# A fourth slot for weight halves, and one slot fewer for gathered rows, in a two-layer decoder step on one core

## The reference

```
h = rmsnorm(x);  proj = h @ w_in                      # 1024 x 2560, and 8 gate columns
mLSTM heads on q, k, v, o;  causal pooling on the last 512 columns
x = x + concat(heads, pooled) @ w_out                 # 1024 x 1024
q = rmsnorm(x) @ wq                                   # 1024 x 2048: 8 heads x 2 halves x 128
s = q . keys;  top 16 of 128 in each half;  top 16 of the 256 sums -> eidx, gate
x = x + sum over 8 heads x 16 experts of gate * gelu(xb . u_tab[eidx]) * v_tab[eidx]
x = x + sigmoid(x @ w_gate) * (p @ w_ple)             # 1024 x 1024, 256 x 1024
```

## Time and profile before

| | |
|---|---|
| median of three runs | 1790.19 us (1785.57 to 1794.6) |
| the profiled execution | 1792.79 us, its span 1790.6 us |
| mean granted TensorE clock | 0.824 |
| PE, DVE, ACT, POOL busy (share of the span) | 76%, 55%, 39%, 28% |
| read from HBM | 679.87 MB |
| mean rate of the DMA engines | 384 GB/s |

### The profile page before, as it was taken

The page is one execution under the profiler, slowest core; times in us unless marked ns, Lnnn a source line. Parts: engine busy times, 40 slices in busy tenths (PEclk is TensorE's granted clock), DMA queues, the critical chain, the costliest instruction groups (busy, mean ns, idle before and its releaser), DMA issues. The chain is left out here.

```text
span 1790.6 us, 19308 instructions
## 1 busy us (share of the span) xinstructions
PE 1364.3 (76%) x6310; PEld 501.9 (28%) x6310; DVE 992.0 (55%) x2540; ACT 692.9 (39%) x1965; POOL 498.0 (28%) x532
## 2 busy tenths in 40 slices
PE   7967689788948879757767897898756677777766
PEld 3523134333413333211113433443311211111113
DVE  1373754756883455875443436668874344555443
ACT  2234435334433453333332645343343333333334
POOL 0031232232222223224332222222333133333330
PEclk9968599889979989986668898899877865676678
DMA  7697699999989999999999799999999989999992
GB/s 309 239 375 306 244 426 428 378 399 426 424 349 377 426 427 417 427 387 392 427 426 422 284 418 421 377 422 416 410 349 427 378 342 427 427 427 427 427 427 116
DMA packets 96737, 687.26 MB, mean 384 GB/s; under 512 B 11104, under 2 KB 12640, under 8 KB 14318
## 3 DMA queue, kind: packets, MB, share of 16 engines
q0 software_dynamic: 76032, 553.68, 74.8%
q1 hardware_dynamic: 20606, 132.36, 18.3%
HBM read 679.87 MB, written 6.59 MB: 383 GB/s over the span
## 5 line engine op out<-in xcount | busy, mean ns | idle before, releaser
L1202 PE MATMUL acc<-rows,weighted 128*64 128x512 f32 x2048 | 699.5, 789 | 268.6 <-ACT weighted L1593 257.2
L2068 DVE SCALAR_TENSOR_TENSOR rows<-rows,shown 128x1024 f32<-128x1024 f32 x528 | 632.7, 1220 | 381.5 <-DMA rows<-in_uv,index_B 249.5
L1399 POOL DMA_INDIRECT rows<-in_uv,index_A x256 | 242.4, 947 | 722.6 <-PE acc L1202 585.7
L889 PE MATMUL bank<-wring,turned 128*128 128x512 f32 (+1 forms) x840 | 385.5, 607 | 8.7 <-DMA wring<-in_w 7.7
L1399 POOL DMA_INDIRECT rows<-in_uv,index_B x256 | 240.4, 939 | 496.6 <-PE acc L1202 474.4
L1202 PEld LDWEIGHTS acc<-rows,weighted 128*64 128x64 f32 x2048 | 134.6, 162 | 731.1 <-ACT weighted L1593 619.7
L889 PEld LDWEIGHTS bank<-wring,turned 128*128 128x128 f32 x840 | 157.7, 196 | 207.6 <-issue 197.3
L1582 ACT ACTIVATE dots_B<-dots_B 128x1 f32<-128x1 f32 x256 | 51.6, 202 | 359.8 <-DVE rows L2068 354.6
L1582 ACT ACTIVATE dots_A<-dots_A 128x1 f32<-128x1 f32 x256 | 51.3, 200 | 267.5 <-DVE rows L2068 253.9
L1593 ACT ACTIVATE weighted<-consts,dots_A 128x64 f32<-128x64 f32 x256 | 89.0, 348 | 8.4
L1593 ACT ACTIVATE weighted<-consts,dots_B 128x64 f32<-128x64 f32 x256 | 89.0, 348 | 8.4
(11 more groups left out here) (312 smaller groups left out, 999.6 us busy)
## 6 DMA issues: line engine op xcount, KB each, us to landing
wring<-in_w SPq DMA_DIRECT2D x107, 1024.0 KB
out_sample<-scratch SPq DMA_DIRECT2D x2, 2128.5 KB, 11.9
scratch<-in_c_s SPq DMA_DIRECT2D x2, 2064.0 KB, 16.0
rows<-in_uv,index_A POOLq DMA_INDIRECT x256
rows<-in_uv,index_B POOLq DMA_INDIRECT x256
keys<-in_keys SPq DMA_DIRECT2D x2, 1024.0 KB
gain<-in_gain SPq DMA_DIRECT2D x3, 640.0 KB
consts<-in_consts SPq DMA_DIRECT2D x1, 1243.0 KB, 11.9
```

The lines of the kernel that those rows point to most:

```text
L889: ins = pe.matmul(ps[:, part], turned["A"][:, 4 * h + c, :], w[:, c, part], start=first, stop=end, skip_group_check=True)
L1202: ins = pe.matmul(acc[c * 64:(c + 1) * 64, :], weighted[:, n % STATS, :], row[:, c * BLOCK:(c + 1) * BLOCK], start=first, stop=end, skip_g ...
L1399: pool.indirect_dma_start(out=rows[:, n % RING, :], out_offset=None, in_=a["uv"], in_offset=bass.IndirectOffsetOnAxis(ap=index[kind][:, pa ...
L2068: dve.scalar_tensor_tensor(u, u, 1.0, shown[:, :, :], ALU.mult, ALU.mult, accum_out=dots[kind][:, part, i:i + 1]).then_inc(u_used, 1)
```

## The change

`RING`, the slots for gathered rows, goes from 8 to 7; `WRING`, the slots for weight halves, from 3 to 4. Both kinds of slot take 8 KB of a partition, so the room is the same. Both numbers also stand in `Clocks`, so the order of stages is made anew by the same rules. The work itself stays the same.

```
-RING = 8
+RING = 7
 STATS = 8
 LANE = 32
 HALF = 2 * P
-WRING = 3
+WRING = 4
```

## The result

The changed kernel takes 1810.55 us (median of 4 runs, 1808.57 to 1812.47) against 1787.88 us for the kernel before beside it: ratio 1.0129, 95% interval 1.0083 to 1.0174, so 23 us slower. The forecast was 1803 with a range of 1785 to 1817. Direction and range hold; the median lies 8 us above the forecast. The profiled execution has a span of 1808.6 us, 18.0 over that of before.

What follows compares the result with a forecast made beforehand. The DMA engines were taken as the bound, with 181 us of lost time to move. Holes 14.8 plus order 3.5 minus start 3.6 minus pass 0 to 1 2.2 made +12.5: forecast 1803 us, range 1785 to 1817.

Steps and rivals of the forecast that it cites:

- A slot less, six holes: DMA holes at 350, 510, 790, 967, 1130, 1290 us: each loses 2.46 us more, sum 14.8, bounds 0 to 17.2.
- What was taken as 0: Pure gather stretches at 0; windows 130 to 220 and 1397 to 1442 us not counted; mixed stretches given no cost.
- The new order: Ranking windows, passes 0 to 2: seven gathers fewer beside the ranking, +3.5 us, bounds -5 to 8.7.
- Start: Before the first index: fourth half already loaded, fifth lands near 29.5, gains 3.6 us, bounds 0 and 4.3.
- Pass 0 to 1: Window 550 to 580 us: fourth half of `gate` resident, PE's wait near 565 gone, gains 2.2 us, low bound 0.
- the two stalls: PE's waits for the fourth half at the start and near 565 us: mending both gives -5.8 us.
- rival (b): 130 to 220 us: new order shortens tile 0's chain by 7 us or more; near 1781, faster; chance 0.14.
- the likeliest case: Whole kernel: gather slots decide, as forecast; own range 1794 to 1816 us; chance 0.55.
- the argument that rests on the pause: SP's pauses in loading halves lie over holes and long stretches, so halves lie ready while gathers are short.
- The signs named beforehand: Changed profile: first gather about 91, no wait near 565, six holes 2 to 3 us larger, 427 GB/s in pure stretches.
- (a): The six holes: room is room, five or more don't grow, only stalls go; 1788 us, no change; chance 0.25.
- (c): Pure gather stretches: seven slots too few, 0.14 us a gather, 36 us in all, 1839 us; chance 0.06.

Runs made afterwards that it cites:

- 7/3: Seven gather slots and three for halves, stage order of the kernel before, against the kernel before: 1821.01 us, ratio 1.0187.
- 7/4: Seven gather slots and four for halves, stage order of the kernel before, against the kernel before: 1817.01 us, ratio 1.0158.
- the limit in one hole: Kernel before (eight and three, its order) with the gather ring seven deep for gathers 104 to 127 only: 1788.03 us, ratio 1.0013.
- the run that limits them: Kernel before with the gather ring seven deep for gathers 32–65, 84–105, 138–189 and 310–349 only: 1802.69 us, ratio 1.0068.
- The second exchange: Six gather slots and five for halves, stage order of the kernel before, against the kernel before: 1863.99 us, ratio 1.0435.
- the run limited in the long stretches: Kernel before with the gather ring seven deep for gathers 208 to 263 and 408 to 527 only: 1786.16 us, ratio 1.0005.

## Why the prediction was right, and where its sum wasn't

*A slot less, six holes, +14.8.* The mechanism was right: the ring is the reserve of the DMA, and a hole that empties it costs one slot more. With the order kept, these holes (gathers 66 to 82, 106 to 136, 190 to 208, 264 to 286, 286 to 318, 350 to 370) lose 1.9 + 4.9 + 2.1 + 0 + 4.6 + 3.0 = 16.5 us more with seven slots (mean of the runs 7/3 and 7/4) than the mean with eight, and the limit in one hole cost 3.0 us of DMA time. Single holes were off: 106 to 136 cost two slots, the one at the pass end showed nothing within its scatter, and its 15.7 us in the profile of before were themselves at the upper end of a scatter from 11.4 to 16.5.

*What was taken as 0.* This is the step of the sum that failed: "Not counted: 130 to 220 [...]; 1397 to 1442" and the silence on the mixed stretches. With the order kept, 0 to 32 and 370 to 410 lose 3.0 and 1.7 us more, and the mixed stretches some 10, shown by the run that limits them and the last gathers of one hole (+12 us, 9.8 us of DMA time in the stretches themselves). I looked for holes in a trace taken with eight slots, and such a trace shows only those deeper than eight slots. Places in which slots come back slower than one in 2.46 us for ten or twenty us, but which eight rows of 2.46 us bridge, look like 427 GB/s there. The second exchange shows that this goes on: 28 us, then 50.

*The new order, +3.5 (bounds -5 to 8.7).* Both signs occur. With eight and three slots it costs 11, over my upper bound of 8.7, which the interval of 7 to 14 still holds; with the slots for which it was made it likely gives back about 5. Put the other way, the exchange of slots costs 28 us in the old order and 12 in the new one (1.0129 against 1.0060). The new order gains in gathers 32 to 82 (6.9 us lost, against 12.6 with the same slots in the order of before) and 330 to 370 (16.4 against 19.1), and loses in 286 to 330 (11.9 against 8.4). I had priced it by gathers leaving the ranking alone, and as a number that doesn't depend on the slots.

*Start, -3.6.* About -2.5. The fifth half came about when the sum had it (29.03, forecast 29.5), with a wait of 1.05 us for it. *Pass 0 to 1, -2.2.* The wait near 565 is gone, but not because of the fourth half: with seven slots and three halves it is gone too. There PE runs from 561.85 to 575.39 with no wait for a load, and under it the run with eight and three slots whose ring is seven deep for gathers 104 to 127, just ahead of this place:

```profile
561.85 13.54 PE L889 MATMUL bank<-wring,turned 128*128 128x512 f32 x31 [0.36 <-issue]
```

```profile
559.16 14.16 PE L889 MATMUL bank<-wring,turned 128*128 128x512 f32 x32 [0.36 <-issue]
```

All four other executions with eight slots in this order wait 2.6 to 3.3 us there. In the limited run the first two of these halves took 6.7 and 5.9 us from issue to landing, in the run limited in the long stretches 10.0 and 9.6: that the halves get more of the DMA when fewer gathers are queued is the likely reason. This term should not have been booked to the half.

*The sum.* Slots with the order kept: 16.5 in the holes, 10 in the mixed stretches, 4.7 in 0 to 32 and 370 to 410, in all 31 us of DMA time; start -2.5, so 28.7, where the time says 28. The order's -5 makes 24, where the time says 23. My +12.5 had the slots 16 us too low, booked 3 us too much to the two stalls and had the order 8 too high. The first two errors point one way and the last the other; that it ended only 10 off is luck.

*The range and rival (b).* The 1816 at the top of the likeliest case adds 17.2 and 8.7 to the median and leaves out the 5.8 us of the two stalls; with them it would have been 1810, just where the measurement lies. The sum of rival (b) takes the order's 3.5 with a minus sign for which it gives no reason; with the plus it comes to 1788, no change. SP's loads before the first pause end at 307 and not near 302 (one more is issued at 306.71); the argument that rests on the pause stands.

*The signs named beforehand.* Right: first gather at about 91, no wait near 565 (for another reason), 427 GB/s in the long stretches, waits for gathers up and for halves down, tail as long (gather 526 lands 35.4 us before the end, 36.3 before). Wrong: the holes by 2 to 3 us each, they changed by -2.5 to +3.0 in the changed kernel. By the prediction's own signs this comes near to "the holes keep their size"; what the holes cost can be seen only with the order kept. *The rivals.* (a) wanted five of six holes that don't grow, and four didn't; but the time rose by 23 us, where (a) had a fall of 2. It said that the extra half is used by the order; that is likely so, at 5 us, and not enough. (b) is out, 0 to 32 lost 2.8 us more. (c) is out.

The Trainium skill (Perfetto Trace Analysis, Optimization Strategy) says that the same gap coming back on the engine that should be saturated can mean too few buffers. The runs agree, with a number (a gather slot: 33 us here, 1.9% of the time), but they show the rule's limit as well: a place without a gap may be living on the last buffer.

## What to carry to other kernels

Before giving a buffer away, don't count the gaps that the profile shows; look at how long the pieces are in which buffers come back slower than the DMA fills them, for those just bridged cost the same slot. A slot has its price at every place where its ring is emptied, and here the price rose with the second slot taken. Which of two rings should get the room showed here in which one is waited for, some 350 us for gathers against 18 for halves; that tells the sign, not the price. A wait that goes away after an exchange need not be mended by what was given: here it went with the gather slot that was taken. An order made by a model for one set of buffers must be timed with these buffers, and not be priced on its own.

## What the runs showed of the hardware

Round trip and rate came apart further than I had thought. In the long stretches a gather takes 13.7 us from issue to landing with eight slots, 11.6 with seven and 8.9 with six, at 427 GB/s in all three (means over gathers 212 to 261): at least the 4.8 us between the first and the last is waiting behind the gathers in front. The product starts 1.6 to 2.1 us after landing and the slot is free 3.9 us after that. So six slots, 14.7 us of transfers, still cover the loop when nothing else runs (0.9 us lost in gathers 208 to 264); the other slots are reserve there.

One profiled execution is a poor ruler for single gaps: with the same instructions, the loss at the pass end lay between 11.4 and 16.5 us, and the start between 32.1 and 36.1.
